# Memory layer: score stores and score loads moved from SyncE's queue to ScalarE's

## The reference

```python
q = (xt @ w_q).reshape(T, 8, 2, 64)
s1, s2 = scores of q against 128 + 128 keys
v1, i1 = top_k(s1, 16); v2, i2 = top_k(s2, 16)
top, pos = top_k(v1 + v2 over all 256 pairs, 16)       # per head
eidx = i1 * 128 + i2 at pos; g = softmax(top)
a = gelu(xt . u_tab[eidx])                             # 8 heads x 16 picks per token
y = sum over picks of g * a * v_tab[eidx]
```

## Time and profile before

| | us |
|---|---|
| median of 3 runs | 3145.73 |
| lowest, highest of them | 3138.82, 3147.31 |
| the profiled execution: its time | 3139.65 |
| its span, first to last instruction | 3137.8 |
| TensorE busy | 2779.3 (89%) |
| VectorE busy | 1446.8 (46%) |
| GpSimd busy | 748.5 (24%) |
| ScalarE busy | 534.6 (17%) |
| TensorE's mean granted clock | 0.947 |

### The profile page before, as it was taken

One profiled execution on the slowest core, in us unless ns is written; L12 is line 12 of the kernel. 1 busy time (PEld: TensorE's weight loads), 2 busy tenths in 40 slices (PEclk: granted clock), 3 DMA queues, 4 the chain that ended last, 5 costly groups with the idle time before them and its releaser, 6 DMA issues. The chain is left out here.

```text
span 3137.8 us, 28344 instructions
## 1 busy us (share of the span) xinstructions
PE 2779.3 (89%) x10072; PEld 1566.3 (50%) x10072; DVE 1446.8 (46%) x2990; ACT 534.6 (17%) x1149; POOL 748.5 (24%) x620
## 2 busy tenths in 40 slices
PE   6999999999997699949889989999866789888877
PEld 3446534456444333324445578888755633333333
DVE  1135200112011322231057249888789977777762
ACT  2024200011001011130147121111122400000011
POOL 0000000000000122110000004456588556555630
PEclk9999998999997799979899999999988999999998
DMA  5101241520123699841300028999999689999981
GB/s 206 54 27 56 108 188 61 221 91 34 54 107 135 242 420 391 340 185 54 115 14 1 27 89 310 408 389 394 374 331 369 218 347 413 413 412 413 413 352 74
DMA packets 142432, 694.17 MB, mean 221 GB/s; under 512 B 20451, under 2 KB 21859, under 8 KB 110563
## 3 DMA queue, kind: packets, MB, share of 16 engines
q1 hardware_dynamic: 59716, 408.31, 33.1%
q0 software_dynamic: 81792, 281.07, 23.1%
q10 hardware_dynamic: 800, 3.15, 0.3%
HBM read 701.89 MB, written 48.23 MB: 239 GB/s over the span
## 5 line engine op out<-in xcount | busy, mean ns | idle before, releaser
L2237 POOL DMA_INDIRECT wring<-in_peer_u,pm_rows x256 | 368.5, 1440 | 736.4 <-DVEq L2530 536.8
L2349 PE MATMUL ps<-hT 128*128 128x512 f32 x1024 | 462.5, 604 | 65.7 <-DVE hT L2554 43.8
L422 PE MATMUL ps<-hT,wring 128*128 128x512 f32 (+2 forms) x1232 | 467.8, 541 | 13.5 <-DMA pm_iota<-in_row_numbers 3.5
L422 PE MATMUL ps<-hT,pm_coef_table 128*128 128x256 f32 x2048 | 451.2, 382 | 0.0
L422 PEld LDWEIGHTS ps<-hT,pm_coef_table 128*128 128x128 f32 x2048 | 392.3, 193 | 53.6
L2560 DVE SCALAR_TENSOR_TENSOR h_tok<-wring,pm_coef,h_tok 128x1024 f32<-128x1024 f32 x256 | 325.0, 1282 | 119.0 <-DMA wring<-in_peer_v,pm_rows 117.4
L2237 POOL DMA_INDIRECT wring<-in_peer_v,pm_rows x256 | 314.0, 1227 | 248.6 <-DVE h_tok L2560 209.8
L2349 PEld LDWEIGHTS ps<-hT 128*128 128x128 f32 x1024 | 189.8, 191 | 337.8 <-issue 232.8
L422 PEld LDWEIGHTS ps<-hT,wring 128*128 128x128 f32 (+1 forms) x1232 | 233.6, 191 | 241.3 <-issue 232.8
L2439 DVE CUSTOM_DVE_ANT_0 wring<-wring,pm_coef_table 128x1024 f32<-128x1024 f32 x256 | 306.0, 1232 | 71.8 <-DMA wring<-in_peer_u,pm_rows 66.6
L1454 POOL COPY ex_idx<-row_token 128x1 uint32 (+1 forms) x24 | 4.5, 186 | 1174.4 <-PEq L1586 1043.7
(11 more groups left out here) (416 smaller groups left out, 2759.6 us busy)
## 6 DMA issues: line engine op xcount, KB each, us to landing
ex_gu<-in_experts SPq DMA_DIRECT2D x32, 2048.0 KB
pm_coef_table<-in_peer_uT SPq DMA_DIRECT2D x64, 1024.0 KB
hT<-in_peer_v SPq DMA_DIRECT2D x64, 1024.0 KB
ex_dn<-in_experts SPq DMA_DIRECT2D x48, 1024.0 KB
wring<-in_w_in SPq DMA_DIRECT2D x21, 2048.0 KB, 8.6
wring<-in_experts SPq DMA_DIRECT2D x16, 2048.0 KB
ada_w<-in_w_ada SPq DMA_DIRECT2D x12, 2048.0 KB
g_dram_out<-pm_coef_table SPq DMA_DIRECT2D x64, 256.0 KB
```

The source lines that it names most:

```text
L422: mm = env.nc.tensor.matmul(out, w[:, k, lo:hi], rhs(k), start=(k == 0), stop=(k == KD - 1))
L2237: nc.gpsimd.indirect_dma_start(ring[n % RING], None, dram[name], bass.IndirectOffsetOnAxis(ap=rows[:, t, j:j + 1], axis=0)).then_inc(got[n ...
L2349: mm = nc.tensor.matmul(env.ps[:, OUT[k], :], W[n % 2][:, at:at + P], vr[p % 2][:, m % 2 * D + k % 2 * WBLK:m % 2 * D + (k % 2 + 1) * WBLK ...
```

## The change

The 64 stores are no longer issued by SyncE. ScalarE issues the store of a pair itself, right after its eviction of the pair's second tile, and waits for its own two evictions first. The loads W(2) to W(31) are issued by ScalarE too, after all its other work in this layer, each behind the same wait on `out_done` as before. W(0) and W(1), all u loads and all v loads stay on SyncE, with their waits.

```diff
--- before.py
+++ after.py
@@ -2244,28 +2244,17 @@
                 nc.sync.dma_start(row, dram["g_ffn_row"].broadcast_to([P, D])).then_inc(row_in, 16)
                 load_blocks(env, sp, 0)
 
-                def store(n):
-                    for t in u_t[2 * n:2 * n + 2]:
-                        evacuated(env, sp, t)
-                    nc.sync.dma_start(dram["g_dram"][n // 2][:, n % 2 * 2 * DS:(n % 2 + 1) * 2 * DS], g[n % GBUF]).then_inc(
-                        g_out[n % GBUF], 16)
-
                 for n in range(PAIRS):
                     if n >= UBUF:
                         product_done(env, sp, u_t[2 * (n - UBUF) + 1])
                     nc.sync.dma_start(u[n % UBUF], dram["peer_uT"][n]).then_inc(u_in[n % UBUF], 16)
-                    if n >= UBUF:
-                        store(n - UBUF)
-                for n in range(PAIRS - UBUF, PAIRS):
-                    store(n)
                 for n in range(GBUF):
                     sp.wait_ge(g_out[n], 16 * PAIRS // GBUF)
                 for t in c_t[EARLY - 1]:
                     product_done(env, sp, t)
                 for n in range(QUADS):
-                    if n >= 2:
-                        sp.wait_ge(out_done, QUAD * (n - 1))
-                    nc.sync.dma_start(W[n % 2], dram["g_dram"][n]).then_inc(w_got[n % 2], 16)
+                    if n < 2:
+                        nc.sync.dma_start(W[n % 2], dram["g_dram"][n]).then_inc(w_got[n % 2], 16)
                     if n == 0:
                         for t in c_t[-1]:
                             product_done(env, sp, t)
@@ -2382,6 +2371,11 @@
                         product_done(env, act, u_t[m])
                         nc.scalar.activation(g[n % GBUF][:, m % 2 * DS:(m % 2 + 1) * DS], env.ps[:, u_t[m][0], 0:DS],
                                              ACT.Gelu).then_inc(env.bank_free[u_t[m][0]], 1)
+                        if m % 2:
+                            for t in u_t[m - 1:m + 1]:
+                                evacuated(env, act, t)
+                            nc.scalar.dma_start(dram["g_dram"][n // 2][:, n % 2 * 2 * DS:(n % 2 + 1) * 2 * DS],
+                                                g[n % GBUF]).then_inc(g_out[n % GBUF], 16)
 
                 def coefficients(n):
                     B = one_hots(n)[1]
@@ -2424,6 +2418,9 @@
                     coefficients(n)
                     if n < EARLY:
                         scores(*beside(n))
+                for n in range(2, QUADS):
+                    act.wait_ge(out_done, QUAD * (n - 1))
+                    nc.scalar.dma_start(W[n % 2], dram["g_dram"][n]).then_inc(w_got[n % 2], 16)
 
             @block.vector
             def _(ve):
```

## The result

The changed kernel is **slower**: 3186.19 us median (3168.21 to 3198.40, 4 runs) against 3143.85 us of the kernel before beside it (4 runs); ratio 1.0133, 95% interval 1.0089 to 1.0178. I had forecast no change, 3146.3 us in a range to 3159, and gave the slower side 0.12.

A forecast was written before the change was run, and what follows sets the result against it. The prediction took TensorE to bound A, GpSimd's issue B and the DMA engines D. Stores +0.6 us, loads 0 and earlier W 0, added to the median 3145.73, gave 3146.3 us; the range took in 3134 and reached 3159.

The forecast's parts named there:

- A: Memory layer, 1890 to 2260 us: the score products run; taken as bound by TensorE, busy 362 of 370 us.
- B: Memory layer, 2260 to 2476 us: remaining score products between coefficient groups; GpSimd's busy time and issue gaps fill 211 of 216.
- D: Memory layer's output, 2520 to 3044 us: taken as bound by the DMA engines at 408 GB/s, 16.35 us per quad.
- The stores: 64 stores issued by ScalarE, taken at 0.5 us each: hidden except for +0.6 us (0.4 to 1.7) before the exponential.
- the joint: End of A: VectorE waits for ScalarE's exponentials behind TensorE's last score tile; the 52nd store adds +0.6 us (0.4 to 1.7).
- B's cover: In B, 12 stores, 7 us in all, fit beside ScalarE's 159 us idle and TensorE's 64.6 us waiting for VectorE: cost 0.
- The loads: the step that failed: In D, v(2n-1) lands 1.3 us later beside W; a quad takes 16.4 us against 16.35: 0 us (0 to 1.6).
- slower rival: In D, the third stream holds v back until TensorE is the bound: up to 37 us slower; chance 0.12.
- edge of 1.25 us: In D, the lateness of v(2n-1) beyond which TensorE becomes the bound: 7.0 + 8.1 + 1.25 = 16.35 us; 1.3 was expected.
- The brake: In D, a late TensorE delays W, VectorE and then the gathers stop, and v has the DMA engines to itself.
- W sooner by 2.4 us: In D, W on its own queue lands at least 2.4 us sooner than today's 10.5; worth 0 us (-2 to 0).
- faster rival: In D, VectorE's waits for W are real losses; five of six shrink by 2.4 us: -12 us, 3134 us; chance 0.07.

The follow-up runs named there:

- the kernel with the gaps filled: The changed kernel plus 12 unused identity products on TensorE ahead of its wait for each odd v; 3155.77 us, ratio 1.0063 to the kernel before.
- the last one: The kernel before with W(n) issued ahead of v(2n-1) on SyncE's queue, plus 12 unused products before each odd-v wait; 3194.94 us, ratio 1.0175.

## Why the prediction was wrong

**The bound of each stage, right.** TensorE in A, GpSimd's issue in B, the bytes in D, with 408 GB/s before.

**The stores, right.** An issue by ScalarE takes 0.338 us, not 0.5. At the joint:

```profile
2257.55 0.38 ACT L2372 ACTIVATE pm_coef_table<-ps 128x256 f32<-128x256 f32 x1 [3.07 <-PE ps L422]
2258.02 0.34 ACTq L2377 DMA_DIRECT2D g_dram_out<-pm_coef_table  x1
2258.39 1.28 ACT L2364 ACT_TABLE_LOAD   x1 [0.46 <-ACT pm_coef_table L2372]
...
2260.02 0.29 DVE L2473 TENSOR_REDUCE pm_coef_table<-pm_coef_table 128x8 f32<-128x128 f32 x1 [24.39 <-ACT pm_coef_table L2364]
```

From the Gelu at 2257.55 to VectorE's restart at 2260.02 are 2.47 us, before 2252.78 to 2254.81, 2.03: +0.44 where I had +0.6. B's cover held:

```profile
PE ps L2304 <- DVE hT L2457: 61.2, 17, 7.2
...
PE ps L2304 <- ACT hT L2384: 1.6, 2, 0.8
...
DVE wring L2436 <- DMA wring<-in_peer_u,pm_rows: 18.7, 16, 3.8
```

TensorE's waits for ScalarE didn't rise (1.6 after 2.4) and its waits for VectorE stayed (61.2 after 64.6).

**The loads: the step that failed** is "TensorE loses the lead that it had and no more: 0 us (0 to 32 x 0.05 = 1.6)". The rule under it held: packets alternate, v has half of the time or a little less. The 9.4 us that I worked out for v are nearly right: the median is 9.3 us in the kernel with the gaps filled and 9.7 in the changed one. But that put a quad at 16.4 us against a limit of 16.35, and I priced the wrong side of that edge as if nothing followed from it. What the runs showed in place of the 0 us: D grew by 55.6 us, TensorE's waits for v from 21.6 to 93.2 us. Two things stand behind it. The first is TensorE's clock. Once TensorE waits some 3 us in every quad, the products after the wait run partly at 1.2 GHz, and those products stand on the chain that issues the next v. The Trainium skill ("TensorE: Matmul & The Clock Gate", What's actually happening) states this as a rule, that the default state is throttled and activity releases it; the trace agrees, 0.50 in the window after the wait and 0.92 over D. The clock was in no term of the sum: from an odd pair's start to the next issue I had 7.0 us, the mean is 8.39, and with the gaps filled 7.12. The products take 28 us more than before, but 42 more than with the gaps filled (448.7 us), as the kernel before has some low clock too, where the bytes are the bound. Filling the gaps took 44 us off D, 578.1 to 533.9. These are the slowest execution of the one kernel and the fastest of the other; by the ratios it is about half of the loss, 1.0133 to 1.0063. The second is the lateness itself, which was mis-sized at the edge: with a full clock a quad takes 16.75 us, not 16.4, and the kernel is still slower by 0.6%. The price of the slower rival had no term for what its own waits would do to the clock.

**The slower rival, right in kind, wrong in size and chance.** Its signs came one by one: waits for v up from 21.6 to 93.2 us, the rate in D to 367, under the 400 that I had named. Its edge of 1.25 us lay below my own 1.3, which is no ground for 0.12. Its upper end, 37 us, counted waiting alone; the runs gave 42 by medians and, with W ahead of v, 97 by the ratio. The 37 us that I called the most were no bound.

**The brake, wrong.** I argued that a late TensorE would stop VectorE and with it the gathers, so that v has the engines to itself. VectorE does stop, for 6.08 us ahead of 2718.58, but gathers are still under way then: from 2713 to 2716, while it stands, their queue had 85 packets to v's 68. W, v and the refill of the ring run together for nearly all of v's way. **W sooner by 2.4 us, wrong:** the median is 9.9 us from issue to landing, 10.2 behind v. It is alone on its queue, but shares the engines with two streams for its whole way (28.1% of the time) instead of with one.

**The faster rival, wrong:** VectorE's waits for W rose from 22.6 to 197.1 us.

## What to carry to other kernels

Two transfers on one queue have an order, and that order may be all that protects the urgent one: before moving the patient one to another issuer, ask which of the two somebody waits for, and keep it behind (same queue, or a wait that lets the urgent one go first). Where a stage is near the edge between two bounds, price what happens past the edge, and add to TensorE's waiting what its clock loses behind each wait: here, by the kernel with the gaps filled, it was about half of the loss. A sum that ends within 0.05 us of the limit says nothing about which side it will be.

## What the runs showed of the hardware

- Three queues with work share the DMA engines packet by packet: 45, 53 and 52 packets in 1.8 us, whatever the bytes of each.
- TensorE's waits of some 3 us, once in 18 us, took the mean clock of the stage from 0.99 to 0.92 in one execution and to 0.95 in another, of the kernel with the loads alone, with the same waiting (0.91 at 3 to 4 us of waiting). Some 2.8 us of products without use in the gap kept it at 1.00 and paid for themselves: 1.0133 to 1.0063.
- Slow stretches of the DMA engines that I can't explain: 324 GB/s at a share of 0.94 in the changed kernel, 313 at 0.93 in the last one, in both with a full clock and VectorE, GpSimd and TensorE all at work. Take every window of 7 us from 10 us after D's first product to 30 us before its last, one for each us, and add up its packets: 23% lie under 345 GB/s in the changed kernel, 18% with the loads alone and 40% with W ahead of v on one queue, against at most 2% where v is spared. So the stretches aren't the second queue's. With filled gaps they fall from 23% to under 1% and from 40% to 15%. What they cost beside the rest, and what sets them off, stays open.
